# One plain 32-bit product in place of three split ones in a two-layer decoder step

## The reference

```
for l in 0, 1:
    x = LN(a*x + mixer(x))             # layer 0: HGRN2, 8 heads; layer 1: GLA, 4 heads
    x = LN(a*x + cross_attention(x))   # 4 heads, memory of 256 tokens; samples have cached K and V
    x = LN(a*x + grouped_moe(x))       # 16 experts in 4 groups, top 2 within the best group

mixer:      proj = x @ w_in ; chunked gated linear recurrence, gated norm ; @ w_out
memory_kv:  kv = mem_prompt @ w_kv     # for the prompt, both layers, also an output
moe:        h = silu(x @ w_gate[e]) * (x @ w_up[e]);  y += combine[:, e] * (h @ w_down[e])
```

## Time and profile before

| | |
|---|---|
| runs | 1377.35 us median of 3 (1375.54 to 1381.28) |
| the profiled execution | 1372.77 us, its span 1371.0 us |
| TensorE, products | 1317.2 us busy (96%), 7570 |
| VectorE / ScalarE | 995.7 us (73%) / 758.8 us (55%) |
| DMA | 356.28 MB, mean 260 GB/s |
| mean granted clock of TensorE | 0.995 of full |

### The profile page before, as it was taken

The page is one execution under the profiler, slowest core; times in us unless marked ns, Lnnn a source line. Parts: engine busy times, 40 slices in busy tenths (PEclk is TensorE's granted clock), DMA queues, the critical chain, the costliest instruction groups (busy, mean ns, idle before and its releaser), DMA issues.

```text
span 1371.0 us, 19477 instructions
## 1 busy us (share of the span) xinstructions
PE 1317.2 (96%) x7570; PEld 1097.6 (80%) x7570; DVE 995.7 (73%) x1078; ACT 758.8 (55%) x777; POOL 201.5 (15%) x240
## 2 busy tenths in 40 slices
PE   8999999999899999999999999999999999999995
PEld 6798997789676888787887799779777788787884
DVE  4456757773568988889995366683558889889894
ACT  4444623523425778687885363332444577777783
POOL 4200246210000000101011014210000000101010
PEclk9999999999999999999999999999999999999998
DMA  9774454346964999999996556434985599999990
GB/s 288 255 268 153 142 183 132 117 151 229 376 240 163 339 363 369 334 363 358 358 379 200 169 165 208 135 121 161 376 318 199 215 363 361 352 372 353 363 365 36
DMA packets 104304, 356.28 MB, mean 260 GB/s; under 512 B 8032, under 2 KB 34160, under 8 KB 74528
## 3 DMA queue, kind: packets, MB, share of 16 engines
q1 hardware_dynamic: 97056, 336.09, 67.6%
q0 software_dynamic: 7168, 19.08, 4.0%
HBM read 334.16 MB, written 26.75 MB: 263 GB/s over the span
## 4 chain that ended last, share of the span: by engine, by line
PE 73%; DVE 11%; ACT 6%; DMA 4%; issue 3%; POOL 2%; SPq 0%; POOLq 0%; DVEq 0%; ACTq 0%
PE ps L1945 59%; DMA att_kt<-in_cache_mem_v 2%; ACT w_hi L897 2%; DVE w_lo L1305 1%; PE ps L2313 1%; PE ps L2336 1%; DVE mix_s L1634 1%; PE ps L2324 1%; PE ps L1954 1%; PE ps L2516 1%; PE ps L1953 1%; PE ps L2055 1%; DVE x L1368 1%; DVE x L1365 1%; DMA raw<-in_xattn_w_kv 1%
## 5 line engine op out<-in xcount | busy, mean ns | idle before, releaser
L1945 PE MATMUL ps<-w_hi,xt_hi 128*128 128x512 f32 x576 | 230.6, 400 | 5.3 <-DVE w_lo L1305 2.2
L1301 DVE TENSOR_TENSOR w_lo<-raw,w_hi 128x2048 fp32r<-128x2048 f32 x62 | 141.4, 2294 | 120.3 <-ACT w_hi L890 120.2
L1945 PE MATMUL ps<-w_hi,xt_lo 128*128 128x512 f32 x576 | 226.3, 393 | 0.0
L1945 PE MATMUL ps<-w_lo,xt_hi 128*128 128x512 f32 x512 | 201.1, 393 | 0.0
L890 ACT ACTIVATE w_hi<-raw 128x2048 fp32r<-128x2048 f32 x64 | 121.8, 1914 | 135.3 <-PE ps L1945 67.3
L1305 DVE TENSOR_TENSOR moe_lo<-moe_in_raw,w_hi 128x2048 fp32r<-128x2048 f32 x72 | 166.0, 2318 | 37.1 <-ACT w_hi L897 37.1
L1305 DVE TENSOR_TENSOR w_lo<-raw,w_hi 128x2048 fp32r<-128x2048 f32 x72 | 164.6, 2289 | 5.7 <-ACT w_hi L897 5.6
L897 ACT ACTIVATE w_hi<-moe_in_raw 128x2048 fp32r<-128x2048 f32 x72 | 137.6, 1920 | 52.8 <-PE ps L1945 52.8
L897 ACT ACTIVATE w_hi<-raw 128x2048 fp32r<-128x2048 f32 x72 | 137.7, 1915 | 12.5 <-PE ps L1945 12.5
L1945 PE MATMUL ps<-xt_hi,w_hi 128*128 128x320 f32 x448 | 138.8, 310 | 0.2
L1945 PE MATMUL ps<-xt_hi,w_lo 128*128 128x320 f32 x448 | 138.6, 309 | 0.0
(11 more groups left out here) (416 smaller groups left out, 2545.0 us busy)
## 6 DMA issues: line engine op xcount, KB each, us to landing
raw<-in_moe_w_gate SPq DMA_DIRECT2D x48, 1024.0 KB, 5.0
moe_in_raw<-in_moe_w_down SPq DMA_DIRECT2D x48, 1024.0 KB, 5.0
moe_in_raw<-in_moe_w_up SPq DMA_DIRECT2D x32, 1024.0 KB, 4.9
raw<-in_moe_w_up SPq DMA_DIRECT2D x32, 1024.0 KB, 5.7
raw<-in_hgrn_w_in SPq DMA_DIRECT2D x16, 1024.0 KB, 5.4
raw<-in_cache_mem_k SPq DMA_DIRECT2D x16, 1024.0 KB, 6.3
moe_in_raw<-in_moe_w_gate SPq DMA_DIRECT2D x16, 1024.0 KB, 5.2
raw<-in_moe_w_down SPq DMA_DIRECT2D x16, 1024.0 KB, 4.8
```

The lines of the kernel that those rows point to most:

```text
L1301: nc.vector.tensor_tensor(lo_at(slot_of(k)), raw_at(slot_of(k)), hi_at(hi_slot(k)).bitcast(F32), ALU.subtract).then_inc(w_low, 1)
L1945: ins = mm(out, lhs, rhs, start=start and n == 0, stop=stop and n == 2, skip_group_check=shared)
```

## The change

Each weight product is made once, from the 32-bit operands as they are. The products, copies and subtractions that served the split go; TensorE waits for the landing of a chunk. `raw` stands where `w_lo` stood; the buffer `w_hi` stays for other uses (heads, values). The recurrence inside the heads keeps its own split parts. Buffers, order of the blocks, loads and stages stay. The memory rows are kept and read back once instead of in two parts. `keep_busy` makes half as many fillers (rounded up), as plain 32-bit products.

```diff
-            def three(out, hi_w, lo_w, hi_x, lo_x, start, stop, x_moves, shared=False):
-                for n, (w, v) in enumerate(((hi_w, hi_x), (hi_w, lo_x), (lo_w, hi_x)) if x_moves else
-                                           ((hi_w, hi_x), (lo_w, hi_x), (hi_w, lo_x))):
-                    lhs, rhs = (w, v) if x_moves else (v, w)
-                    ins = mm(out, lhs, rhs, start=start and n == 0, stop=stop and n == 2, skip_group_check=shared)
-                return ins
+            def product(out, w, v, start, stop, x_moves, shared=False):
+                lhs, rhs = (w, v) if x_moves else (v, w)
+                return mm(out, lhs, rhs, start=start, stop=stop, skip_group_check=shared)
+
+            def weights_in(k, groups):
+                pe.wait_ge(loaded[slot_of(k)], at(16 * loads_of(k), groups, 16 * GCH // MR))
+
+            def tile_products(par, r, kc, kt, t):
+                n = live(t)
+                return product(ps[0:n, 4 * par + t, :], raw[:, r, kc, :], xt[:, kt, t * P:t * P + n], kt == 0, kt == KT - 1, False)
...
-                        pe.wait_ge(w_low, at(base + j + 1, g, GCH))
+                        pe.wait_ge(loaded[j % MR], at(16 * moe_loads_of(l, j), g, 16 * GCH // MR))
...
 (VectorE, head_out)
-                    nc.vector.tensor_tensor(m["y"][:], m["y"][:], m["rn"][:]...to_broadcast([P, VB, NT]), ALU.mult).then_inc(hd_y, 1)
-                    dve.wait_ge(hd_hi, n + 1)
-                    nc.vector.tensor_tensor(xt_lo[:, rows, 0:NT], m["y"][:], xt_hi[:, rows, 0:NT].bitcast(F32), ALU.subtract)
-                    nc.vector.tensor_tensor(xt_hi[:, rows, NT:TILES * P], m["y"][:, :, PROMPT:NT], ..., ALU.subtract).then_inc(hd_fin, 1)
+                    nc.vector.tensor_tensor(xt[:, h * VB:(h + 1) * VB, 0:NT], m["y"][:], m["rn"][:]...to_broadcast([P, VB, NT]), ALU.mult).then_inc(hd_fin, 1)
 (VectorE, add_tile)
-                if t == 2:
-                    link(ins)
-                    ins = nc.vector.tensor_tensor(cols, cols, ps[64:P, 4 * (db % 2) + t, :], ALU.add)
 (ScalarE and VectorE: split, split_expert, split_next, split_ahead and all their calls)
-                nc.scalar.activation(hi_at(hi_slot(k)), raw_at(r), ACT.Copy).then_inc(w_high, 1)
-                nc.vector.tensor_tensor(lo_at(slot_of(k)), raw_at(slot_of(k)), hi_at(hi_slot(k)).bitcast(F32), ALU.subtract).then_inc(w_low, 1)
 (TensorE, keep_busy)
-                rows = r_hi[:].rearrange("p k e -> p (k e)")
-                for n in range(count):
+                rows = router[:].rearrange("p k e -> p (k e)")
+                for n in range((count + 1) // 2):
```

More of the change, by code:

```diff
@@ L421, in value_at, with mem_rows @@
             return st_att["kt"][:, (4, 0, 1, 2)[n - 5]].rearrange("p c m -> p (c m)").rearrange("p (a m) -> p a m", a=4)
[L423 to L430, removed]
+        def mem_rows(db):
+            return st_kv["rows"] if db < KV_BLOCKS[0] else st_moe["mem"]
         def kv_staged(db):
@@ L552, in _ @@
             dense(3, 2 * KV_BLOCKS[0], None)
-            sp.wait_ge(xt_l, 8)
-            for part in range(2):
-                sp.dma_start(mem_rows_kept[part], st_kv[("mem_hi", "mem_lo")[part]][:].bitcast(F32)).then_inc(mem_in[part], 16)
+            sp.wait_ge(xt_in, 8)
+            sp.dma_start(mem_rows_kept, st_kv["rows"][:]).then_inc(mem_in[0], 16)
             done = 2 * KV_BLOCKS[0]
@@ L572, in _ @@
                 if l == 1:
-                    for part in range(2):
-                        sp.wait_ge(mem_in[part], 32)
-                        sp.dma_start(late_mem[part].bitcast(F32), mem_rows_kept[part]).then_inc(mem_in[part], 16)
+                    sp.wait_ge(mem_in[0], 32)
+                    sp.dma_start(st_moe["mem"][:], mem_rows_kept).then_inc(mem_in[0], 16)
                 if l == 1:
@@ L1046, in _ @@
                     act.wait_ge(kv_out[par], kv_outs(l))
-                for part in range(2):
-                    act.wait_ge(mem_in[part], 32)
+                act.wait_ge(mem_in[0], 32)
                 def decay_args():
@@ L1182, in _ @@
                 rows_out(0)
-                splits[0] = chunk_no(db + 4)
-                split(splits[0], groups)
-                splits[0] += 1
                 rows_out(1)
@@ L1188, in _ @@
                 rows_back(1)
[L1189 to L1193 removed]
+                layer_norm(3 * l + 1, 3 + 3 * l)
                 m, s = st_moe, mo[l]
[L1196 to L1198 removed]
                 act.wait_ge(rt_ps, 2 * l + 1)
@@ L1369, in tile_norm, with block_norm @@
                                                op0=ALU.mult, op1=ALU.add).then_inc(ln_done, 1)
-            def turned(u, t):
-                n = live(t)
-                per = NB // n
-                for half in range(KT // per):
-                    dve.wait_ge(xt_h, turns(u, t) + half + 1)
-                    hi = xt_hi[:, per * half:per * (half + 1), t * P:t * P + n]
-                    nc.vector.tensor_tensor(xt_lo[:, per * half:per * (half + 1), t * P:t * P + n],
-                                            ps[:, turn_bank0(u, t) + half, :].rearrange("p (k s) -> p k s", s=n), hi.bitcast(F32), ALU.subtract).then_inc(xt_l, 1)
-            def block_norm(db, groups, q, u):
+            def block_norm(db, groups, q):
                 par = db % 2
@@ L1454, in _ @@
                     dve.wait_ge(kv_out[par], kv_outs(l))
-                for part in range(2):
-                    dve.wait_ge(mem_in[part], 32)
+                dve.wait_ge(mem_in[0], 32)
                 def scan(hh):
@@ L1911, in _ @@
                 ins.then_inc(rt_comb, 1)
-                for j in range(2, MH):
-                    split_expert(base + j, j, g0)
                 visit(0, True, False)
@@ L1924, in _ @@
                 row_norm(nl + 1)
-                if l == 0:
-                    splits[0] += NH
-                    for n in range(2):
-                        split(splits[0], groups)
-                        splits[0] += 1
-                    for t in range(TILES):
-                        turned(4, t)
-                    dve.wait_ge(xt_l, turns(4, 2) + 1)
-                    samples_pad(xt_lo[:, :, PROMPT:NT].bitcast(F32))
-                    split_ahead(BLOCKS0 + 1, groups)
         @block.tensor
@@ L2243, in _ @@
                     for kt in range(KT):
-                        ins = three(ps[0:16, 7, 0:NT], lr_hi[:, kt, :], lr_lo[:, kt, :], xt_hi[:, kt, 0:NT], xt_lo[:, kt, 0:NT], kt == 0, kt == KT - 1, True)
+                        ins = product(ps[0:16, 7, 0:NT], w_lr[:, kt, :], xt[:, kt, 0:NT], kt == 0, kt == KT - 1, True)
                     ins.then_inc(mx_lr, 1)
@@ L2428, in _ @@
                 block_norm(db + 5, groups, 3 * l + 1, 3 + 3 * l)
-                pe.wait_ge(rt_w, 2)
                 for kt in range(KT):
-                    ins = three(ps[0:EXPERTS, 4, 0:TILES * P], r_hi[:, kt, :], r_lo[:, kt, :], xt_hi[:, kt, :], xt_lo[:, kt, :],
-                                kt == 0, kt == KT - 1, True)
+                    ins = product(ps[0:EXPERTS, 4, 0:TILES * P], router[:, kt, :], xt[:, kt, :], kt == 0, kt == KT - 1, True)
                 ins.then_inc(rt_ps, 1)
@@ L2544, in turn_next @@
                                 ins.then_inc(xt_ps, 1)
-                    for part in range(2):
-                        pe.wait_ge(mem_in[part], 48)
+                    pe.wait_ge(mem_in[0], 48)
                     pe.wait_ge(evac[0], db // 2)
```

421 lines of the change are left out of this document (94 added, 327 removed).

## The result

The changed kernel takes 1667.97 us (median of 4 runs, 1667.53 to 1668.81) against 1379.32 us before in the same comparison (4 runs, 1375.54 to 1382.37): the ratio is 1.2095, with a 95% interval of 1.206 to 1.213. The forecast was 1116 us with a range of 1080 to 1195. It was wrong in sign and by 552 us. What came is the rival that had a chance of 0.04, about 1630 us.

The account below looks back on a forecast made before the run. TensorE was taken as the bound, the DMA a few per cent behind in the expert stages. 77 + 35 + 20 + 19 + 8 + 6 + 7 + 97 - 8 = 261 us off 1371.0 gave 1110, put at 1116 us; range 1080 to 1195.

Parts of the forecast that it names:

- the price of a plain product: Everywhere in the kernel: a plain product takes 0.427 us at 512 columns, 0.270 at 320; three split ones 0.693, 0.444.
- The double-price rival: Whole kernel: a plain product costs 0.854 us at 512 columns, 0.540 at 320; about 1630 us, slower; chance 0.04.
- T blocks: 14 blocks, weights stationary, 320 tokens moving (f, q, k, gate, attention q): 14.2 to 8.6 us each, 77 us off.
- visit: Expert stages: 24 chunks of four products, some 47 us against 72; 88 us at 0.854 us a product.
- The terms that depend on the DMA: Mainly the expert stages: loads at 406 GB/s, 239 us a layer in place of 288.2 and 287.4, 97 us off.
- the first keys and values: Memory keys and values at the start, six blocks: done at 62 to 63 us, 19 us off.
- the 0.65 us of a shorter chain: Heads of layer 0: state updates that release the next head come some 0.65 us sooner; heads 8 us over both layers.
- All that making the parts costs: Terms outside the products: norms 12, heads 8, routing 6, between the layers 7, together 33 us off.
- The N blocks' term: 12 blocks: eight (v, first output-projection halves) 4.3 us off each, 35; four beside the layer norm 5 each, 20.
- The rival of a low clock: Expert stages: the clock falls in gaps between chunks and stays down, a layer 352 us, total 1342 us; chance 0.08.

Follow-up runs that it names:

- two passes: Changed kernel with two 16-bit products on the upper halves (second with a zero stationary tile) per weight product, low halves left out, half the fillers: 1143.05 us.
- one pass: Changed kernel with one 16-bit product on the upper halves per weight product, low 16 bits left out, half the fillers: 1060.99 us.

## Why the prediction was wrong, point by point

**The step that failed: the price of a plain product.** I took a record for a product. The groups of the earlier trace rows are pairs: the program issues four products at L2209, and the row says x8; the "two of 512 columns in 1.02 us" were one product. The other group, L2324, has 64 records in the trace for 32 products. So 0.427 us was the spacing of half products, and the price is 0.858 at 512 columns and 0.538 at 320, twice my 0.427 and 0.270. The sentence "the trace disagrees" came of the same misreading. One plain product costs 0.858 / 0.680 = 1.26 times its three split ones at 512 columns alone, and 0.858 / 0.693 = 1.24 times in the kernel, where I had 0.62. By the Trainium skill (FP8 and Floating Point Precision, TensorE Precision Notes) true FP32 takes four passes; the measured 0.858 against 0.224 for a 16-bit product is 3.8 times. I had both groups' counts before me and multiplied none of them out against the program.

**The double-price rival.** Its T blocks came exactly: 34.47 / 2 = 17.2 us, 14.2 + 3.0. Its visit of 88 us is 86.8. It ended 38 us low. Two things that it left out are measured: the widths of the third tile, 16 us, and the fillers, which it kept at half the number and my price; with a quarter of them 34 us came back. Its visit was 1.2 us too long, 10 us over eight. These overlap with chains and with the rounding of its terms, so they are not a sum to the microsecond.

**The terms that depend on the DMA** were right at the price assumed: 231 us an expert stage against 239, the DMA share of 1 and over 400 GB/s, the two f blocks in 17.9 us (two times 8.6 forecast), the first keys and values done at 64.5 us against 62 to 63. At the real price, the DMA share is 0.83 and 0.80 and none of it shows.

**The chains beside VectorE and ScalarE.** One is mis-sized. In the kernel with two passes the chain shows a head of layer 0 every 7.29 us against 7.51 before, so the 0.65 us of a shorter chain is 0.22. All that making the parts costs, for which I had 33 us, comes to about 25 to 30 by the estimate above. The N blocks' term left out that a 64-column tile costs extra between tiles of 128.

**The clock.** The rival of a low clock failed in its place: at two passes the clock stayed at 1.00 in the expert stages. Its mechanism was seen at one pass, at 0.77, and cost next to nothing there. By the Trainium skill (TensorE: Matmul & The Clock Gate, HAM oscillation) bursts cut by waits for the DMA run throttled again and again; the run at one pass agrees with its 0.77, the run at two, at 1.00, does not show it.

**The range and the chances.** A step on which 515 us hung got a chance of 0.04 because two groups agreed; but both were read the same way, so they were one piece of evidence.

## What to carry to other kernels

Before a row gives the price of an instruction, multiply out how many of it the program issues and divide by the count of records: one plain 32-bit product leaves two. A plain product replaces three split ones at a gain only at 192 columns or fewer in these measurements (with 128 stationary ones); at 512 the splits on ScalarE and VectorE lay mostly beside TensorE's work and saved it a fifth of the price. And when a change reprices an instruction, price every use of it, fillers too.

## What the runs showed of the hardware

- A plain 32-bit product is recorded twice, each record with half its time: 0.429 us at 512 columns, 0.216 at 256, 0.112 at 128.
- A change of the stationary width between 128 and 64 columns cost 0.17 us in a run of plain 32-bit products and 0.11 us with 16-bit ones, at 512 moving columns; between split products it cost nothing. Padding the tile to 128 made the changed kernel 16.3 us faster.
- The granted clock fell without a gap between records: to 0.62 over the group of three split products of 96 columns, and to 0.63 over plain ones of 32, while plain ones of 96 and 64 columns ran at 1.00. What tells them apart is open.
- The DMA gave 419 GB/s over a whole expert stage, more than the 411 that I had seen at best.
